# Dense units of the first attention set between the transposes of the probabilities and the product with the values

## The reference, cut to what matters

```python
s = jnp.einsum('bqhgd,bkhd->bhgqk', qi, k_all).astype(jnp.float32) * ATTN_SCALE
p = jax.nn.softmax(s, axis=-1)
attn = jnp.einsum('bhgqk,bkhd->bqhgd', p.astype(v_all.dtype), v_all)
...
conv = jax.nn.silu(layernorm(y, ln_g, ln_b))          # y: gated, depthwise convolution
mix = jnp.concatenate([attn * jax.nn.silu(za), conv * jax.nn.silu(zb)], axis=-1)
x_new = x + gate * (mix @ ev_w_out[e])
```

## Time and profile before

| | us |
|---|---|
| median of 3 runs | 3133.24 (3131.53 to 3140.49) |
| the profiled execution, its own time | 3135.02 |
| its span, first to last instruction | 3133.2 |
| mean granted clock of TensorE | 0.922 |
| busy in the span: TensorE, VectorE, ScalarE, GpSimd | 2721.6, 2060.1, 611.2, 905.2 |
| stretch of the first attention, scores of head 0 to the output projection | 392.4 to 504.2 |

### The profile page before, as it was taken

One profiled execution on the slowest core, in us unless ns is written; L12 is line 12 of the kernel. 1 busy time (PEld: TensorE's weight loads), 2 busy tenths in 40 slices (PEclk: granted clock), 3 DMA queues, 4 the chain that ended last, 5 costly groups with the idle time before them and its releaser, 6 DMA issues.

```text
span 3133.2 us, 31368 instructions
## 1 busy us (share of the span) xinstructions
PE 2721.6 (87%) x12124; PEld 2187.7 (70%) x12124; DVE 2060.1 (66%) x2774; ACT 611.2 (20%) x1226; POOL 905.2 (29%) x724
## 2 busy tenths in 40 slices
PE   5998989999999999999999999446566766999996
PEld 4786768888888788877888888446566665444442
DVE  5878965737535437612563238999998879656667
ACT  1011031110010110012100021111157778000000
POOL 0110001101000000000110004567776666556664
PEclk9999999999999999989999999778777776999998
DMA  9994457949877633322797439999999998999998
GB/s 376 392 395 145 166 211 308 388 147 372 353 276 296 272 121 108 114 101 81 313 422 297 148 136 418 378 380 412 421 417 387 385 385 253 384 404 409 414 413 348
DMA packets 148876, 951.38 MB, mean 304 GB/s; under 512 B 16528, under 2 KB 16528, under 8 KB 50320
## 3 DMA queue, kind: packets, MB, share of 16 engines
q0 software_dynamic: 103680, 620.80, 49.4%
q1 hardware_dynamic: 43920, 320.65, 26.6%
q10 hardware_dynamic: 1152, 8.26, 0.7%
HBM read 945.45 MB, written 4.19 MB: 303 GB/s over the span
## 4 chain that ended last, share of the span: by engine, by line
PE 49%; DVE 19%; DMA 17%; ACT 6%; issue 4%; POOL 4%; DVEq 0%; ACTq 0%; POOLq 0%
PE G L448 40%; DMA acc<-v_rows,proj 6%; DMA mix<-v_rows,proj 3%; DMA aring<-ada 3%; DVE vec L1976 3%; DVE aring L1948 2%; ACT vec L1216 2%; PE M L890 2%; DVE ring L1948 2%; DVE proj L1436 2%; DVE proj L1606 2%; DVE aring L1353 1%; PE G L878 1%; DMA ring<-peer_u,proj 1%; DMA vec<-peer_u,proj 1%
## 5 line engine op out<-in xcount | busy, mean ns | idle before, releaser
L448 PE MATMUL G<-h,ring 128*128 128x256 f32 x4864 | 1072.2, 382 | 14.2 <-ACT h L974 14.2
L448 PEld LDWEIGHTS G<-h,ring 128*128 128x128 f32 x4864 | 930.6, 192 | 147.1 <-issue 18.2
L407 POOL DMA_DIRECT2D aring<-ada x208 | 109.9, 530 | 1579.5 <-DVE mods L1353 1573.1
L1353 DVE CUSTOM_DVE_ANT_0 aring<-aring,acc,vec 128x2048 f32<-128x2048 f32 x176 | 410.3, 2350 | 139.1 <-DMA aring<-ada 137.7
L448 PE MATMUL G<-proj,ring 128*128 128x256 f32 x2080 | 456.7, 382 | 0.9 <-DVE proj L1827 0.9
L448 PEld LDWEIGHTS G<-proj,ring 128*128 128x128 f32 x2080 | 398.3, 192 | 57.2 <-issue 2.0
L422 POOL DMA_INDIRECT aring<-peer_u,proj x128 | 217.7, 1701 | 312.6 <-DVE proj L1914 190.6
L931 PE MATMUL M<-sq,mix 128*128 128x512 f32 x688 | 299.0, 592 | 1.2 <-ACT mix L1230 1.2
L1948 DVE CUSTOM_DVE_ANT_0 aring<-sq,aring 128x2048 f32<-128x2048 f32 x108 | 245.3, 2290 | 31.1 <-DMA aring<-peer_u,proj 20.8
L942 ACT ACTIVATE proj<-G 128x256 f32<-128x256 f32 (+1 forms) x168 | 64.5, 384 | 995.7 <-PE G L448 995.6
L1976 DVE SCALAR_TENSOR_TENSOR vec<-acc,dots,vec 128x1024 f32<-128x1024 f32 x149 | 191.2, 1283 | 99.0 <-DMA acc<-v_rows,proj 92.9
(11 more groups left out here) (345 smaller groups left out, 2873.0 us busy)
## 6 DMA issues: line engine op xcount, KB each, us to landing
ring<-weights SPq DMA_DIRECT2D x217, 1024.0 KB, 5.4
aring<-ada POOLq DMA_DIRECT2D x208, 1024.0 KB, 12.2
sq<-v_blocks SPq DMA_DIRECT2D x43, 1024.0 KB, 8.1
proj<-v_blocks SPq DMA_DIRECT2D x21, 1024.0 KB, 8.1
ring<-first SPq DMA_DIRECT2D x16, 1024.0 KB, 8.3
acc<-v_rows,proj POOLq DMA_INDIRECT x151, 9.7
x<-xT SPq DMA_DIRECT2D x1, 2048.0 KB, 12.1
acc<-conds ACTq DMA_DIRECT2D x2, 1024.0 KB, 11.3
```

The lines of the kernel that those rows point to most:

```text
L407: pool.dma_start(aring[:, n % SLOTS, :], ada[a]).then_inc(ada_in[n % SLOTS], 16)
L448: mm = nc.tensor.matmul(bank[:, 0:TOK], lhsT=ring[:, slot, weights_at + t * P:weights_at + (t + 1) * P], rhs=rhs[:, t, :], start=(t == ord ...
L1353: V_.tensor_tensor_reduce(out=tile, in0=tile, in1=vector, scale=1.0, scalar=bias, op0=ALU.mult, op1=ALU.add, accum_out=column).then_inc(ad ...
```

## The change

In the call of the first attention an empty dictionary is passed for `between`, and the dictionary of calls that stood there becomes `copying`. So TensorE issues each head's interleaved work after the transposes and before it waits for ScalarE's copy, and the product with the values comes behind it. The programs of ScalarE, VectorE, SyncE and GpSimd are as they were, and so is the second attention, which passes both dictionaries already.

```diff
             attention(0, 4, lambda hh: proj[:, hh, :], lambda hh: kv_keys[:, hh // 4, :],
                       lambda hh, kt: vtok[:, kt * 256 + (hh // 4) * P:kt * 256 + (hh // 4 + 1) * P],
-                      sq[:, 2048:3072], False,
+                      sq[:, 2048:3072], False, {},
                       {0: lambda: zb(2), 1: conv_mean, 3: zb_after_mean, 4: conv_variance,
                        5: lambda: zb(4), 6: zb_after_variance, 7: lambda: zb(6, 2)})
```

## The result

The change makes the kernel slower: 3148.0 us median (3138.4 to 3152.8, 12 runs) against 3132.3 (3128.1 to 3140.5, 12 runs), a ratio of 1.0049 with a 95% interval of [1.0039, 1.0058]. The 15.7 us stand against the 16.3 of the sum; the forecast of 3150 lies 2 us above.

The account below looks back on a forecast made before the run. TensorE was taken to set the pace; moving the work uncovers VectorE's chain. 7.8 us without the clock, 3.4 for short gaps and 5.1 for long ones make +16.3, given as 3150 us, range 3141 to 3158.

Parts of the forecast that it names:

- the sum: First attention, all heads: 7.8 us without the clock, 3.4 for short gaps, 5.1 for long gaps, together +16.3 us.
- The chain: VectorE from product to next probabilities, hidden by the dense unit: the copy wait of 1.1 us becomes one of 2.3.
- Head 3: First attention's head 3: period 14.6 us against 14.44, +0.2, including 0.8 left of its cold start.
- Head 7: Last head, to the output projection: 20.2 us against 22.27, -2.1, with a 4.6 us gap ahead of the projection.
- The clock: TensorE drops from 2.4 to 1.2 GHz after gaps, 1.7 us a drop: +3.4 for short gaps, +5.1 for long.
- The three long gaps: TensorE gaps of 4.1, 4.1 and 4.6 us (last ahead of the projection): a clock drop in each, +5.1 us.
- a drop in two of the four: Short gaps of about 2.3 us behind heads 0, 1, 3 and 4: two drop the clock, +3.4 us.
- The row at 164.45: Profile row after a 3.20 us gap: 8 matmuls in 1.97 us, full rate, evidence against a drop in short gaps.
- the one at 1230.36: Profile row after a 2.21 us gap: 16 matmuls in 5.41 us against 3.72, evidence for a 1.7 us drop.
- the +7.8 without the clock: First attention's heads: period changes of 3.7, 0.2, 3.05, 2.95 and -2.1 us, before any clock drop.
- the rival of the absorbed delay: Stages after 504 us take up the loss: 3133 us, give or take 9; chance 0.1.
- The rival on the other side: VectorE's chain fits under the scores, so only the copy wait goes: -8.7 us, 3124.5; chance 0.04.

Follow-up runs that it names:

- e1: Changed kernel, with VectorE's second ada tile (heads 0, 1, 3, 4, 6, 7) and head 5's scaling ahead of the wait for the product: 3121.6 us, ratio 0.9963.
- e3: Changed kernel, with both ada tiles (head 5: its one) put behind the product on VectorE: 3171.7 us, ratio 1.0125.
- e2: Kernel before the change, TensorE order untouched, with the same VectorE move as e1: 3131.2 us, ratio 1.0000.
- e6: Changed kernel, interleaved work spread over other heads, all ada tiles, centring, scaling and gates' product ahead of VectorE's wait: 3113.0 us, ratio 0.9946.
- e4: Kernel before the change, with only head 7's two units moved ahead of the product: 3130.2 us, ratio 0.9995.

## Why the prediction was right

**The chain.** The argument was that the wait for the copy goes and a longer one for VectorE's probabilities comes. The list of waits shows it (12.2 to 1.1, and 4.7 to 22.2), e1 and e3 shorten and lengthen it by a tile, and e2 shows that the unit's cover is what had made it free.

**The terms, from copy to copy.** Head 0: 13.76 measured, 13.83 in the sum. Heads 1 and 4: 419.00 to 429.31 and 456.61 to 466.92, 10.31 each for 10.38. Head 2, to which nothing was to happen: 11.49, the same as before. Head 5: 482.56 - 466.92 = 15.64 for 15.66. Head 3 was mis-sized: 456.61 - 440.80 = 15.81 for 14.6, because its cold start cost the unit 2.1 us (9.16 for 7.07) on top of the 0.9 in the transposes, where the sum had 0.8. Its own rows already said more than the 1.7 that it gave to this cold start: the transposes' 0.9 and, for the product of 3.78 instead of 1.99, another 1.8, so 2.7. Head 6 (498.85 - 482.56 = 16.29) is 13.83 and 1.7 for the clock that was billed apart, and another 0.8 in cold transposes. Head 7 (521.06 - 498.85 = 22.21) is 20.2 and 2.0 lost in its units.

**The clock** is the term whose size was off, in both directions. *"The three long gaps ... a drop in each, +5.1"*: the drops came, in all three traces, but at 1.7 us only the first was priced right. The one in head 7 cost 0.9 + 2.1 = 2.9 (transposes of 1.97 for 1.09, a pair of units of 16.05 for 13.98). The one ahead of the projection cost 2.9 too: its first unit is read by ScalarE 531.08 - 521.06 = 10.0 us after its first matmul, where before it was 511.34 - 504.17 = 7.2. The two reads, before and after:

```profile
511.34 0.47 ACT L942 ACTIVATE h<-G,mods 128x256 f32<-128x256 f32 x1 [6.58 <-PE G L448]
...
531.08 0.47 ACT L942 ACTIVATE h<-G,mods 128x256 f32<-128x256 f32 x1 [16.00 <-PE G L448]
```

That makes 7.5 for 5.1. The sum took the price of a drop behind a gap of 2.21 us for the long gaps too, though its own rows priced the one of 4.69 at 2.7. *"I take a drop in two of the four"*: it was 0, 3 and 1, which by the periods cost 0, 3.5 and 1.7 us, 1.7 on average instead of 3.4. The row at 164.45 and the one at 1230.36 were both fair witnesses: a gap of 2 to 3 us may or may not cost. The rule of the Trainium skill that was weighed ("TensorE: Matmul & The Clock Gate", section "Loop structure matters more than you think": a VectorE copy between bursts "doesn't break PE warmth") fits eight of the twelve gaps and not the other four.

**What was luck.** The clock's two errors (1.7 us too much for the short gaps, 2.4 too little for the long ones) and head 3's 1.2 work partly against each other, so that the whole came within 1 us of the measured difference owes something to chance; the +7.8 without the clock doesn't. Of the signs that were named, one didn't show in the first trace: the granted clock of the stretch was to fall under 0.92 and was 0.93 there (0.88 and 0.90 in the other two). And the projection's first matmul, forecast at 519 to 522 us, came at 521.06 only because this execution was 5.0 us late at the first scores; by its stretch alone it would be 516.1.

**The whole.** From the first copy to the projection it was 504.17 - 401.58 = 102.6 before and 521.06 - 405.24 = 115.8 in the first trace of the change, +13.2; the first scores' own cold start, 1.3 us, which before had and this execution hadn't, makes it the 11.9 of the stretch. The three traces of the change have stretches of 123.7, 128.9 and 127.1, 126.6 on average; the two traces with TensorE's order of before (before and e2) have 111.8 and 113.6. That is +13.9, and 2.9 behind it in the projection's first unit: 16.8, beside a difference of the medians of 15.7. From the projection's first matmul to the last instruction the three traces take 2629.9, 2631.2 and 2629.1 us, the trace of before 2629.0 and e2's 2621.4. A delay that was taken up later would have made this part some 14 us shorter with the change, and it isn't, though it scatters by some 10 us; nor does the difference of the whole, whose interval begins at 12 us, leave room for it. So the rival of the absorbed delay is out. In the first of them TensorE is busy without a break for 110.5 us behind the stretch, as before.

**The rival on the other side** was named with its condition: faster if the next probabilities were ready 3.7 us after the product's start, break-even at 4.8, some 3124.5 us. e1 makes just that condition, by moving the 2.28 us of the tile, and lands at 3121.6, 9.2 us under the kernel before beside it, where this rival had 8.7. What the change lacked was not the idea but the other half.

## What to carry to other kernels

Before independent work is moved into one wait, look at what it hides where it stands: here it covered 4 us of VectorE's chain between the product and the next probabilities, and was moved to cover a copy of 1 us. Both fit under it, if what doesn't depend on the product (ada tiles, scaling) is put ahead of VectorE's wait for the product; the two edits only pay together (e1, against the change alone and e2). A period written down from the trace, instruction by instruction round the loop, gave each head to 0.1 us where the clock stayed up. What a drop of the clock costs behind a long gap has to be read behind a gap of that length, not behind a short one.

## What the runs showed of the hardware

The same gap of TensorE, 2.32 us, at the same place in the same kernel, was followed by half clock in four of twelve cases (in one of them a wait of 1.11 us lay between) and by full clock in the others; together with the gap of 3.00 us at L565 that makes 5 us of difference between the stretches of one kernel (123.7 to 128.9). That gap of 3.00 us, which is there in all ten traces, was followed by half clock in nine of them. Gaps of 1.76 and 2.40 us (e1, e6) were not. Gaps of 4.04 us and more in this stretch were followed by half clock every time in the ten traces, at a cost of 1.4 us (e3, head 5) to 3.8 (e4, head 3: transposes 1.97 for 1.04, product 3.78 for 1.99, unit 8.15 for 7.07) each. How much work then runs at half clock is not the same either, which the sum had taken for one number: behind head 3's wait of 4.70 us the unit took 9.16 us in one trace of the changed order and 8.72 in another (e1).
